# Few-frequency products of a depthwise convolution in column and row groups, its mean by sum columns, and a norm loop in which two engines write the operand

## The reference

```python
def conformer_conv(h, pw1_w, pw1_b, dw_w, dw_b, ln_g, ln_b, pw2_w, pw2_b):
    a, g = jnp.split(h @ pw1_w + pw1_b, 2, axis=-1)
    u = a * jax.nn.sigmoid(g)
    u = depthwise_conv(u, dw_w) + dw_b          # 31 taps along the tokens, each of 1024 channels alone
    u = jax.nn.silu(layernorm(u, ln_g, ln_b))   # mean and variance over the 1024 channels
    return u @ pw2_w + pw2_b
```

## Time and profile before

| | us |
|---|---|
| median of 3 runs | 963.69 |
| lowest, highest | 962.48, 964.80 |
| span of the profiled execution (first to last instruction) | 957.4 |
| TensorE busy in it | 902.7 (94%) |
| VectorE busy | 737.5 (77%) |
| ScalarE busy | 468.4 (49%) |
| GpSimd busy | 137.7 (14%) |

### The profile page before, as it was taken

How to read it: one execution, slowest core, us unless ns; L and a number is a source line. 1 busy time by engine, 2 the same in 40 slices (tenths; PEclk the granted TensorE clock), 3 DMA queues, 4 the chain that set the end, 5 groups by cost and what they waited for, 6 DMA issues and landing times.

```text
span 957.4 us, 12493 instructions
## 1 busy us (share of the span) xinstructions
PE 902.7 (94%) x4323; PEld 711.5 (74%) x4323; DVE 737.5 (77%) x1074; ACT 468.4 (49%) x783; POOL 137.7 (14%) x204
## 2 busy tenths in 40 slices
PE   3899999989999999899989999999979999999996
PEld 1588766767888888677667788888867777878874
DVE  1598689888768677879689797678698888976674
ACT  2462358555343444563275434434445876545651
POOL 0001130405001211040001510020001110101000
PEclk9899999999999999999999999999999999999998
DMA  9987743559998889557525699898857446795001
GB/s 351 386 344 269 280 151 122 170 179 352 370 316 289 313 287 321 191 161 245 195 89 197 231 395 333 278 337 297 280 183 271 132 164 210 247 360 183 24 23 44
DMA packets 121238, 229.09 MB, mean 239 GB/s; under 512 B 8666, under 2 KB 64700, under 8 KB 121194
## 3 DMA queue, kind: packets, MB, share of 16 engines
q1 hardware_dynamic: 94800, 141.57, 42.4%
q0 software_dynamic: 24224, 86.32, 25.7%
q10 hardware_dynamic: 2170, 0.64, 0.3%
HBM read 227.43 MB, written 1.08 MB: 239 GB/s over the span
## 4 chain that ended last, share of the span: by engine, by line
PE 73%; DVE 13%; issue 5%; ACT 4%; DMA 2%; POOL 1%; SPq 0%; ACTq 0%; DVEq 0%; POOLq 0%
PE bank L2162 21%; PE bank L2164 20%; PE bank L2163 20%; PE bank L2745 1%; DVE w_lo L1425 1%; DVE job_sum L1311 1%; DMA x<-x_dram 1%; DMA w_land<-ev_w_in_dram 1%; DVE x L1376 1%; DVE w_lo L1294 1%; DVE tmp L1375 1%; PE bank L2583 1%; PE bank L2243 1%; ACT w_hi L724 1%; PE bank L2656 1%
## 5 line engine op out<-in xcount | busy, mean ns | idle before, releaser
L2162 PE MATMUL bank<-w_hi,xT_hi 128*128 128x512 f32 x784 | 316.1, 403 | 12.0 <-DVE xT_lo L1952 4.4
L2164 PE MATMUL bank<-w_hi,xT_lo 128*128 128x512 f32 x784 | 307.9, 393 | 0.0
L2163 PE MATMUL bank<-w_lo,xT_hi 128*128 128x512 f32 x784 | 307.2, 392 | 0.0
L1294 DVE TENSOR_TENSOR w_lo<-w_land,w_hi 128x2048 fp32r<-128x2048 f32 x107 | 246.9, 2312 | 77.1 <-ACT w_hi L724 77.0
L724 ACT ACTIVATE w_hi<-w_land 128x2048 fp32r<-128x2048 f32 x107 | 204.5, 1915 | 109.3 <-PE bank L2164 100.6
L2162 PEld LDWEIGHTS bank<-w_hi,xT_hi 128*128 128x128 f32 x784 | 148.5, 189 | 49.8 <-issue 14.4
L2164 PEld LDWEIGHTS bank<-w_hi,xT_lo 128*128 128x128 f32 x784 | 148.1, 189 | 32.2
L2163 PEld LDWEIGHTS bank<-w_lo,xT_hi 128*128 128x128 f32 x784 | 148.7, 190 | 28.2
L1311 DVE SCALAR_TENSOR_TENSOR job_sum<-a_land,silu_c,job_sum 128x1024 f32<-128x1024 f32 x126 | 162.3, 1288 | 6.4 <-DMA a_land<-mod_w_dram 2.6
L2162 PE MATMUL bank<-w_hi,hT_hi 128*128 128x512 f32 x176 | 69.9, 397 | 2.8 <-DVE hT_lo L1773 2.8
L2164 PE MATMUL bank<-w_hi,hT_lo 128*128 128x512 f32 x176 | 68.7, 390 | 0.0
(11 more groups left out here) (338 smaller groups left out, 1148.4 us busy)
## 6 DMA issues: line engine op xcount, KB each, us to landing
w_land<-ffn_w_dram SPq DMA_DIRECT2D x132, 512.0 KB, 5.4
a_land<-ada_w_dram POOLq DMA_DIRECT2D x40, 1024.0 KB, 5.8
a_land<-mod_w_dram POOLq DMA_DIRECT2D x24, 1024.0 KB, 6.6
w_land<-od_pw_w_dram SPq DMA_DIRECT2D x24, 512.0 KB, 5.1
w_land<-ev_w_in_dram SPq DMA_DIRECT2D x20, 512.0 KB, 10.6
w_land<-ada_w_dram SPq DMA_DIRECT2D x16, 512.0 KB, 9.8
a_land<-kv_mod_w_dram POOLq DMA_DIRECT2D x8, 1024.0 KB, 6.6
w_land<-rg_w_in_dram SPq DMA_DIRECT2D x16, 512.0 KB, 5.0
```

What stands on the lines that cost most here:

```text
L1294: dve.tensor_tensor(w_lo[PLACE[u]][:, :], w_land[n % N_LAND][:, :], w_hi[PLACE[u]][:, :].bitcast(F32), ALU.subtract).then_inc(s_lo, 1)
L2162: pe.matmul(dst, hi, whi, start=start, stop=False)
L2163: pe.matmul(dst, hi, wlo, start=False, stop=False)
L2164: return pe.matmul(dst, lo, whi, start=False, stop=stop)
```

## The change

It does four things. `to_few` runs once, for all four chunks, behind `to_waves(3)`, and `few_times_taps` once, on all 128 rows. The products of `few_z` leave `from_waves` and come last, in `from_few`: four row groups into four banks, first for e = 0, then for e = 1. The mean's products swap their roles: VectorE scales `ones` by a column of `z_sum` (`mean_cols`, 128 x 128), and TensorE multiplies it with `back`. In the norm loop VectorE itself writes `xT_hi` for the steps n = 2, 5, 8, 11 and 14, and `split_lo(pw2+2)` moves from ahead of the loop to behind it. `job_sums(9)` now stands between `to_few` and `from_waves(3)`, and the two steps of `job_units(10, (0,))` stand together behind the third mean column.

```diff
PRODUCT = {"part": 2}
+LN_DVE_HI = (2, 5, 8, 11, 14)
 STEPS = [("n_x", WHOLE), ("n_ctx", {**WHOLE, "full": 4, "act_full": 4}),
...
          ("out", PRODUCT), ("n_ffn0", TILED), ("ffn0", {"part": 3}), ("n_pw1", TILED),
-         ("ln", {"full": 2 * KT, "hi": 2 * KT, "lo": 2 * KT}), ("pw2", PRODUCT),
+         ("ln", {"full": 2 * KT, "hi": 2 * KT - len(LN_DVE_HI), "lo": 2 * KT}), ("pw2", PRODUCT),
          ("n_ffn1", TILED), ("ffn1", {"part": 3}),
...
         conv = place("conv", [P, KT, S], S1)
-        mean_waves = place("mean_waves", [P, 3, S], BIG)
+        mean_cols = place("mean_cols", [P, 3, P], BIG + 29 * KB)
         bias_gate = place("bias_gate", [P, D], BIG + 34 * KB)
...
                                bias=pc("od_ln_b", k)).then_inc(sem("full"), 1)
-                act.wait_ge(*seen("full", "ln", n + 1))
-                act.activation(xT_hi[:, k, cols], xfull[:, k, cols], ACT.Copy).then_inc(sem("hi"), 1)
+                if n not in LN_DVE_HI:
+                    act.wait_ge(*seen("full", "ln", n + 1))
+                    act.activation(xT_hi[:, k, cols], xfull[:, k, cols], ACT.Copy).then_inc(sem("hi"), 1)
             dense_out("pw2", "n_ffn1", 8)
...
-            def few_times_taps(n, rows, after):
-                dve.wait_ge(sem("few_mm"), n + 1)
-                dve.wait_ge(sem("conv_z"), after)
-                dve.tensor_tensor(prod[rows, :], bank[7][rows, :], few_spec[rows, :], ALU.mult).then_inc(sem("few_prod"), 1)
-                dve.wait_ge(sem("few_prod"), n + 1)
-                dve.scalar_tensor_tensor(out=few_z[rows, :], in0=prod[rows, 0:256], scalar=1.0, in1=prod[rows, 256:512], op0=ALU.mult,
-                                         op1=ALU.add, accum_out=z_sum[rows, 10:11]).then_inc(sem("conv_few_z"), 1)
+            def few_times_taps():
+                dve.wait_ge(sem("few_mm"), 1)
+                dve.wait_ge(sem("conv_z"), 8)
+                dve.tensor_tensor(prod[:, :], bank[7][:, :], few_spec[:, :], ALU.mult).then_inc(sem("few_prod"), 1)
+                dve.wait_ge(sem("few_prod"), 1)
+                dve.scalar_tensor_tensor(out=few_z[:, :], in0=prod[:, 0:256], scalar=1.0, in1=prod[:, 256:512], op0=ALU.mult,
+                                         op1=ALU.add, accum_out=z_sum[:, 10:11]).then_inc(sem("conv_few_z"), 1)
+            def mean_col(n):
+                dve.tensor_scalar(mean_cols[:, n, :], ones[:, :], z_sum[:, 8 + n:9 + n], None, ALU.mult).then_inc(sem("ln_mean_cols"), 1)
...
             times_taps(1)
-            few_times_taps(0, slice(0, 64), 4)
             split_lo(pw1 + 8)
             job_units(9, (2,))
-            dve.wait_ge(sem("conv_few_z"), 1)
             times_taps(2)
-            few_times_taps(1, slice(64, 96), 6)
             split_lo(pw1 + 9)
...
             glu(3)
-            job_units(10, (0,), None, (0,))
-            dve.wait_ge(sem("conv_few_z"), 2)
             times_taps(3)
-            few_times_taps(2, slice(96, 128), 8)
-            dve.wait_ge(sem("conv_few_z"), 3)
-            for n, col in enumerate((8, 9, 10)):
-                dve.tensor_scalar(mean_waves[:, n, :], back[:, n, :], z_sum[:, col:col + 1], None, ALU.mult).then_inc(sem("ln_mean_waves"), 1)
-            job_units(10, (0,), None, (1,))
+            mean_col(0)
+            mean_col(1)
+            few_times_taps()
+            dve.wait_ge(sem("conv_few_z"), 1)
+            mean_col(2)
+            job_units(10, (0,))
             dve.wait_ge(sem("ln_mean"), 1)
...
             for k in range(KT):
-                dve.wait_ge(sem("conv_mm"), 2 * (k // 2) + 2)
+                dve.wait_ge(sem("conv_mm"), 5 + k // 2)
                 dve.scalar_tensor_tensor(out=conv[:, k, :], in0=bank[(6, 0, 1, 2)[k // 2]][:, 256 * (k % 2):256 * (k % 2) + 256],
...
             job_units(10, (1,), None, (0,))
-            split_lo(BASE["pw2"] + 2)
             dve.wait_ge(sem("ln_std"), 1)
...
                 k, cols = n % KT, slice(n // KT * P, n // KT * P + P)
-                dve.wait_ge(*seen("hi", "ln", n + 1))
+                if n in LN_DVE_HI:
+                    dve.wait_ge(*seen("full", "ln", n + 1))
+                    link(dve.tensor_copy(xT_hi[:, k, cols], xfull[:, k, cols]))
+                else:
+                    dve.wait_ge(*seen("hi", "ln", n + 1 - sum(m < n for m in LN_DVE_HI)))
                 dve.tensor_tensor(xT_lo[:, k, cols], xfull[:, k, cols], xT_hi[:, k, cols].bitcast(F32),
...
                     link(dve.reciprocal(rln[:, cols], rln[:, cols]))
-                dve.wait_ge(sem("ln_xc"), k + 1)
+                dve.wait_ge(sem("ln_xc"), KT)
                 dve.tensor_tensor(csq[:, k, cols], conv[:, k, cols], rln[:, cols], ALU.mult).then_inc(sem("ln_norm"), 1)
...
                 ln_low(n)
+            split_lo(BASE["pw2"] + 2)
             job_units(10, (1,), None, (1,))
...
-            def to_few(groups, free):
-                pe.wait_ge(*free)
+            def to_few():
+                pe.wait_ge(sem("dw_bias_sums"), 1)
                 for h in range(2):
                     for t in range(NT):
-                        for g in groups:
+                        for g in range(4):
                             ins = pe.matmul(bank[7][32 * g:32 * g + 32, 256 * h:256 * h + 256], few_waves[:, t, 32 * h:32 * h + 32],
...
                 pe.wait_ge(sem("conv_z"), 2 * c + 2)
-                if c < 3:
-                    pe.wait_ge(sem("conv_few_z"), max(c, 1))
                 if c == 1:
...
                     pe.wait_ge(sem("pw1_ag"), 8)
-                r = slice(32 * c, 32 * c + 32)
                 for e in range(2):
-                    if (c, e) == (3, 1):
-                        pe.wait_ge(s_rows, rows_upto(9))
-                        for n in range(3):
-                            pe.wait_ge(sem("ln_mean_waves"), n + 1)
-                            ins = pe.matmul(bank[4][:, 0:S], ones[:, :], mean_waves[:, n, :], start=n == 0, stop=n == 2)
-                        ins.then_inc(sem("ln_mean_mm"), 1)
-                    dst = bank[(6, 0, 1, 2)[c]][:, 256 * e:256 * e + 256]
                     cols = slice(256 * c + P * e, 256 * c + P * e + P)
-                    pe.matmul(dst, z_re[:, cols], back[:, 0, :], start=True, stop=False)
-                    pe.matmul(dst, z_im[:, cols], back[:, 1, :], start=False, stop=False)
-                    if (c, e) == (3, 0):
-                        pe.wait_ge(sem("conv_few_z"), 3)
-                    pe.matmul(dst, few_z[r, P * e:P * e + P], back[r, 2, :], start=False, stop=True).then_inc(sem("conv_mm"), 1)
+                    pe.matmul(wave_half(c, e), z_re[:, cols], back[:, 0, :], start=e == 0, stop=False)
+                    pe.matmul(wave_half(c, e), z_im[:, cols], back[:, 1, :], start=False, stop=False)
+            def wave_half(c, e):
+                return bank[(6, 0, 1, 2)[c]][:, 256 * e:256 * e + 256]
+            def mean_sums():
+                pe.wait_ge(s_rows, rows_upto(9))
+                for n in range(3):
+                    pe.wait_ge(sem("ln_mean_cols"), n + 1)
+                    ins = pe.matmul(bank[4][:, 0:S], mean_cols[:, n, :], back[:, n, :], start=n == 0, stop=n == 2)
+                ins.then_inc(sem("ln_mean_mm"), 1)
+            def from_few():
+                pe.wait_ge(sem("conv_few_z"), 1)
+                for e in range(2):
+                    for c in range(4):
+                        r = slice(32 * c, 32 * c + 32)
+                        pe.matmul(wave_half(c, e), few_z[r, P * e:P * e + P], back[r, 2, :],
+                                  start=False, stop=e == 1).then_inc(sem("conv_mm"), 1)
...
                     to_waves(2)
-                    to_few((2,), (sem("conv_few_z"), 1))
                     from_waves(0)
...
                     to_waves(1)
-                    pe.wait_ge(sem("spec_out"), 5)
-                    to_few((0, 1), (sem("dw_bias_sums"), 1))
...
             from_waves(2)
+            to_waves(3)
+            to_few()
             job_sums(9)
-            to_waves(3)
-            to_few((3,), (sem("conv_few_z"), 2))
             from_waves(3)
+            mean_sums()
+            from_few()
             for k in range(KT):
...
```

## The result

| | before | after |
|---|---|---|
| median of 4 executions each | 963.09 us (960.07 to 964.80) | 950.73 us (950.53 to 952.02) |
| ratio, 95% interval | | 0.9884 [0.9862, 0.9907] |
| span of the profiled execution | 957.4 us | 950.3 us |
| time of that execution | (not on record) | 952.02 us |

The change makes the kernel 1.2% faster. The prediction was 954.5 us with a range of 952.7 to 958.0; the measured 950.73 lies 3.77 us under the forecast and 2.0 under the range. The direction was right, the size was not.

What follows compares the result with a forecast made beforehand. TensorE, busy 94% of the span, was taken to bound the kernel. 2.05 + 5.34 + 1.18 + 1.30 + 1.50 - 2.20 = 9.17 us gained; span 948.2 plus 6.3 gave 954.5 us, range 952.7 to 958.0.

Steps and rivals of the forecast that it cites:

- 6.3 us over the span: Final step: median 963.69 over the 957.4 span, taken as untouched, so the predicted 948.2 span became 954.5 us.
- rival 3: More won: Silus at 0.22 us (1.05 more), ScalarE not holding the mean (0.55): 952.9 us; chance 0.05.
- first few products of pw1: Few-frequency products of chunks 0 and 1 removed inside pw1: 1.85 plus 0.20 of switching, 2.05 us gained.
- second ones, and every third product of the way back: Before pw1's last unit: chunk 2's few products and from_waves of chunks 0 and 1 become eight full products, 5.34 us gained.
- end of pw1 to the conv values: Stretch of 11.89 us becomes 10.71, with ScalarE's chain before the mean now binding: 1.18 us gained.
- conv values to the first Silu: Norm before its loop: with split_lo(pw2+2) moved away, first Silu 6.54 us after conv start, not 7.84: 1.30 us gained.
- norm loop: ScalarE bounds the loop; five of sixteen Copies go to VectorE, Silus 0.43 us apart there: 1.50 us gained.
- moved split: split_lo(pw2+2) queued behind the loop delays VectorE's rest for pw2+3; all of it counts: -2.20 us.
- switch of 0.20 us: On TensorE, each change between a full array and a part of it was said to cost 0.20 us.
- rival 1: from_few's row groups run one after the other: only 7.65 to 6.85 us gained, 956.0 to 956.8 us; chance 0.13.
- whether the clock stays at 2.4 GHz or falls only changes how long TensorE waits for pw2+3: In pw2 after TensorE's pause: VectorE's chain decides pw2+3, ready at 496.72 us; TensorE there at 495.7, waiting 1.0 us.
- Rival 2: Gain partly taken back before the mean, in the norm loop, at pw2+3 or in ffn1: 955.7 to 959.2 us; chance 0.12.

Runs made afterwards that it cites:

- experiment 1: Kernel before, unchanged, run again against itself: 962.15 us median of 10 executions beside 961.76 of 23; profiled execution 962.30 us, span 960.6.
- experiment 2: Kernel before, unchanged, two more profiled executions: 964.20 us with a span of 962.5, and 962.05 us with a span of 960.4.
- experiments 5 to 9: Kernel after with old norm part; unshared copies; from_few chunk by chunk; split_lo(pw2+3) before residual; that plus six unused products: 953.74, 953.06, 952.45, 952.82, 952.73 us.
- experiment 4: Kernel before with only the norm part added (shared xT_hi writes, split_lo(pw2+2) behind the loop): 960.80 us, ratio 1.0003.
- experiment 7: Kernel after with from_few walking chunk by chunk, each pair of conv values waiting for its own chunk: 952.45 us, ratio 0.9909.
- experiment 8: Kernel after with split_lo(pw2+3) ahead of the first residual, in pw2 alone: 952.82 us, ratio 0.9904.
- experiment 10: Kernel after, one half step of job 10 moved to ffn1, its freed load moved back on GpSimd's queue: 957.81 us; with six unused TensorE products 958.55 us.

## Why the prediction was wrong, point by point

**The step that failed** is the last one: "Against the median of 963.69 (6.3 us over the span, which the change doesn't touch) that is 954.5". No row showed 6.3 us outside the span. What lies outside is 1.7 (experiment 1). The other 4.6 are time inside the span that the median execution loses and the traced one does not: in stretches at 1.2 GHz and, in two of the four traces of before, in a wait of TensorE in ffn1 (experiment 2). The sum was made on one execution and added to the median of others.

Of the 3.77 us, 1.5 are that the median of three lay above the 962.2 of 77, 0.4 that the first four executions of after lay below the 951.2 of all eight, and 1.8 that the gain between these medians is 11.0 and not 9.17. Of this 1.8, 1.1 goes away when executions of one mean clock are compared (9.9). The 0.8 that is left stays open; the time times the mean clock scatters by 1.4 us from one execution of a kernel to the next, and 8 executions of after don't settle it. One candidate, not shown, is the wait in ffn1: 1.40 and 1.86 us in two traces of before and none in the other two, 0.31 and none in the two of after, and at most 0.58 in those of experiments 5 to 9. The mean clock does not see it. But that of experiment 4, with the convolution of before, has none either, and so few traces don't prove that the change shortens it.

On its own execution the sum would have given 948.2 + 1.7 = 949.9, which is 0.8 under the measured 950.73. That this is near is in part luck, as the spans show. The span fell by 7.1 us, not by the 9.0 that the changed stretch gained. Before the stretch the trace of after was already 0.92 us late: it has a stretch at 1.2 GHz at 218 to 222 us (1.6) that the trace of before lacks, and lacks one at 44 us that this one has. Behind the stretch it lost 0.6 at and behind the wait of 0.31 in ffn1, and 0.4 near 710, where its stretch at 1.2 GHz is 6.8 us long and that of before 3.4. To put the change's worth between the two spans would have been as wrong.

**The range** had no term for this. It took in each bound of the change and none of the baseline, whose 77 executions spread over 8 us. Its lower end, 952.7, was called the far end of rival 3, which by its own sum is 952.9.

**The terms of the sum**, with the shift of the third chunk's end taken off:

| term | predicted | measured |
|---|---|---|
| first few products of pw1 | 2.05 | 2.06 |
| second ones, and every third product of the way back | 5.34 | 5.35 |
| end of pw1 to the conv values | 1.18 | 0.90 |
| conv values to the first Silu | 1.30 | 1.27 |
| norm loop | 1.50 | 1.61 |
| moved split | -2.20 | -2.19 |
| sum | 9.17 | 9.00 |

One term was mis-sized, the third. ScalarE's chain came as reckoned (table load when the mean's sum is ready), but from_few ends last, not ScalarE. Its fifth signal was put 0.9 us behind its start, 0.2 ahead of the end of the two rounds. VectorE started 1.2 behind it, since the products of a round end together (experiment 7). The mean alone would have let it start some 0.3 us earlier: it stood 0.75 us behind the start of `mean`, where it stood 0.42 behind it in the kernel before. The Silus were 0.39 apart instead of 0.43, at the end named for overlap.

The switch of 0.20 us was read rightly: with no few products beside them, the full products behind to_waves take 0.43 each in the kernel after. In the kernel before, inside pw1, it stands on both sides of each few product (L2693):

```profile
457.32 0.43 PE bank L2690 x2
457.75 0.62 PE bank L2693 x2
458.38 0.63 PE bank L2689 x2
```

**Row groups** ran side by side, so rival 1 fell: 1.15 to 1.20 us for eight products, where 3.44 to 4.96 was its price. The Trainium skill (TensorE: Matmul & The Clock Gate, "The cost: per-tile semaphore tail") would put some 273 ns behind eight signals, an estimate from its formula. VectorE started at the fifth signal, and no row here shows when the eighth came, so the trace does not settle that estimate.

**The clock** behind the pause: "whether the clock stays at 2.4 GHz or falls only changes how long TensorE waits for pw2+3" held for the kernel as it is, with the traced stretch of 3.4 us. It is not general. With a stretch of 6.8 us TensorE frees a weight buffer so late that ScalarE and VectorE wait too (experiment 8), and with VectorE 1.2 us earlier it was TensorE that set the end (experiment 10).

**Rival 2**, a part taken back in the ffn1 loop, came only as the 0.6 us named above, but experiment 10 shows that its size was real: 5.2 us there from one moved transfer. The prediction let the shift carry through since "TensorE's waits to the end name no transfer". That reading looked one step back only: TensorE waits for VectorE's `w_lo`, and VectorE for a_land ahead of it (experiment 2). The forecast's own line "I am wrong if the shift at pw2+3 is not the one at the end" was met only in part: the shift went from 8.1 to 7.1, by a stretch at 1.2 GHz and the wait in ffn1, with no change in the order of work.

## What to carry to other kernels

Make the sum against the execution that was traced and know its time; to go from there to a median, take the spread of the executions as a term of its own, with both ends. An edit of a few us is read from a stretch of the trace between two fixed products, not from the two totals. Before a step is moved, look at what stands behind its transfers in an in-order queue: a load that waits 3 us there cost 5 us some 35 us later, 3.7 as a wait and the rest as a stretch at 1.2 GHz behind it. And when the chain names an engine, look at what that engine waited for.

## What the runs showed of the hardware

Stretches at 1.2 GHz come at a few places (near 20, 44, 118, 220, 404, 420, 481 to 493, 557 to 561 and 706 to 718 us, and at the very end), but not all of them in every execution, and not equally long. At 418 to 428 us the kernel before ran at full clock in three traces and at 1.2 GHz in one, for 6.8 us, which cost 3.2. Behind the same pause of 4.4 us the stretch was 3.4 us long in three traces of the kernel before and 6.8 in one. Behind one of 3.2 us, with the changed norm loop, it was 3.4 us long in four traces, 6.8 in three and missing in one (experiment 4). In executions of the unchanged kernel before, the time went from 961 us at a mean clock of 0.986 to 964 at 0.980 or 0.981, and one with 0.986 and a wait of 1.86 us in ffn1 took 962.05.

Four column groups (32 records) cost what one costs (8 records): 1.86 and 1.84 us. Four row groups in four banks run side by side whatever order they are issued in: 1.15 and 1.17 us. Going from the full array to part of it costs 0.20 us, and going back another 0.20.
